# Where the copies of the smaller caches are issued in a decoder step on one core

## What is computed

```
h = RMSNorm(x) * (1 + scale1) + shift1
q_nsa, kv_nsa, g_nsa, qkv_dil, g_merge = split(h @ w_in)
o_nsa, o_dil = NSA attention, dilated attention (three head groups)
m = sigmoid(gA) * (o_nsa @ w_br_nsa) + sigmoid(gB) * (o_dil @ w_br_dil)
x = x + gate1 * (m @ w_out)
h = RMSNorm(x) * (1 + scale2) + shift2
x = x + gate2 * ((silu(h @ w_gate) * (h @ w_up)) @ w_down)
y = RMSNorm_final(x)
```

```
s_win  = concat(cache_win,  new)[:, 1:]   # 8 samples x  512 rows x  256 floats
s_dil1 = concat(cache_dil1, new)[:, 1:]   # 8 samples x  128 rows x 1024 floats
s_dil2 = concat(cache_dil2, new)[:, 1:]   # 8 samples x  512 rows x 1024 floats
s_dil3 = concat(cache_dil3, new)[:, 1:]   # 8 samples x 2048 rows x 1024 floats
```

## Time and profile before

| | |
|---|---|
| median of 3 runs | 2106.77 us (2106.63 to 2110.05) |
| profiled execution | 2110.02 us, of it 2107.7 us span from first to last instruction |
| TensorE busy | 1952.0 us, 93% of the span |
| VectorE, ScalarE busy | 977.2 us (46%), 772.9 us (37%) |
| granted TensorE clock, mean | 0.950 |
| moved by DMA | 512.53 MB, 243 GB/s on average |

### The profile page before, as it was taken

How to read it: one execution, slowest core, us unless ns; L and a number is a source line. 1 busy time by engine, 2 the same in 40 slices (tenths; PEclk the granted TensorE clock), 3 DMA queues, 4 the chain that set the end, 5 groups by cost and what they waited for, 6 DMA issues and landing times.

```text
span 2107.7 us, 36811 instructions
## 1 busy us (share of the span) xinstructions
PE 1952.0 (93%) x15765; PEld 1786.1 (85%) x15765; DVE 977.2 (46%) x1730; ACT 772.9 (37%) x1232; POOL 58.4 (3%) x108
## 2 busy tenths in 40 slices
PE   6988999999879997999999996999999999999967
PEld 3667999999645565699999996999999999999966
DVE  3355445554346532264444756344444433645425
ACT  2345333334324432253333434333333333533322
POOL 0000000000000000000000000000000000000010
PEclk9998989999989959889999997999999999999989
DMA  9981769889899916665555653686767676578791
GB/s 372 422 288 61 214 208 313 280 275 301 338 393 372 412 43 251 229 191 186 180 182 170 219 172 141 235 271 230 267 231 267 233 244 207 196 243 270 249 315 56
DMA packets 336137, 512.53 MB, mean 243 GB/s; under 512 B 8753, under 2 KB 310105, under 8 KB 319497
## 3 DMA queue, kind: packets, MB, share of 16 engines
q1 hardware_dynamic: 316146, 368.53, 52.5%
q0 software_dynamic: 5248, 125.73, 15.1%
q10 hardware_dynamic: 14640, 16.80, 2.4%
HBM read 504.29 MB, written 98.91 MB: 286 GB/s over the span
## 4 chain that ended last, share of the span: by engine, by line
PE 84%; DMA 9%; DVE 4%; ACT 2%; issue 1%; SPq 0%; DVEq 0%; ACTq 0%
PE bank L1129 17%; PE bank L1130 17%; PE bank L1131 17%; PE bank L842 5%; PE bank L843 5%; PE bank L844 5%; DMA piece<-in_w_ada 4%; PE bank L732 3%; PE bank L769 2%; DMA piece<-in_w_down 2%; PE bank L900 2%; PE bank L875 1%; DMA mem<-in_cache_sel_kv,runs 1%; DMA mem<-in_const 1%; PE bank L888 1%; PE bank L960 1%
## 5 line engine op out<-in xcount | busy, mean ns | idle before, releaser
L1129 PE MATMUL bank<-piece,piece 128*128 128x264 f32 x3072 | 877.8, 286 | 50.6 <-DVE piece L2050 26.0
L1130 PE MATMUL bank<-piece,piece 128*128 128x264 f32 x3072 | 877.0, 285 | 0.0
L1131 PE MATMUL bank<-piece,piece 128*128 128x264 f32 x3072 | 876.6, 285 | 0.0
L2055 DVE TENSOR_TENSOR piece<-piece,piece 128x2048 fp32r<-128x2048 f32 (+2 forms) x216 | 440.9, 2054 | 504.5 <-ACT piece L1541 504.5
L1129 PEld LDWEIGHTS bank<-piece,piece 128*128 128x128 f32 x3072 | 582.4, 190 | 52.2 <-DVE piece L2055 24.6
L1541 ACT CAST piece<-piece 128x2048 fp32r<-128x2048 f32 (+2 forms) x216 | 368.7, 1715 | 589.0 <-PE bank L1131 509.6
L1131 PEld LDWEIGHTS bank<-piece,piece 128*128 128x128 f32 x3072 | 582.4, 190 | 0.0
L1130 PEld LDWEIGHTS bank<-piece,piece 128*128 128x128 f32 x3072 | 582.0, 189 | 0.0
L842 PE MATMUL bank<-piece,piece 128*128 128x264 f32 (+1 forms) x816 | 241.1, 295 | 0.0
L843 PE MATMUL bank<-piece,piece 128*128 128x264 f32 (+1 forms) x816 | 234.9, 288 | 0.0
L844 PE MATMUL bank<-piece,piece 128*128 128x264 f32 (+1 forms) x816 | 234.5, 287 | 0.0
(11 more groups left out here) (324 smaller groups left out, 1449.7 us busy)
## 6 DMA issues: line engine op xcount, KB each, us to landing
piece<-in_w_ada SPq DMA_DIRECT2D x48, 2048.0 KB, 12.3
out_s_dil<-in_cache_dil_kv POOLq DMA_DIRECT2D x64, 1023.5 KB, 6.3
piece<-in_w_in SPq DMA_DIRECT2D x50, 1024.0 KB, 8.2
piece<-in_w_gate SPq DMA_DIRECT2D x22, 2048.0 KB, 8.1
piece<-in_w_up SPq DMA_DIRECT2D x22, 2048.0 KB, 8.1
piece<-in_w_down SPq DMA_DIRECT2D x32, 1408.0 KB, 6.7
piece<-in_w_in SPq DMA_DIRECT2D x16, 2048.0 KB, 8.2
piece<-in_w_out SPq DMA_DIRECT2D x8, 2048.0 KB, 8.7
```

What stands on the lines that cost most here:

```text
L1129: mm(out, w_high[:, k, :], half_tile(x_high[k]), start=(start and k == first_tile), stop=False)
L1130: mm(out, w_high[:, k, :], half_tile(x_low[k]), start=False, stop=False)
L1131: last = mm(out, w_low[:, k, :], half_tile(x_high[k]), start=False, stop=(stop and k == len(x_high) - 1))
L2055: v.tensor_tensor(half_chunk(a, k_tiles, f, CW), raw, half_chunk(buffer, k_tiles).bitcast(F32), ALU.subtract)\
```

## The change

GpSimd's list of copies is put in another order, with other waits. The `dil2` copies come directly behind the selected gathers, and the copy of sample c waits for `mg_half` 1 + 6c, the first half of iteration c of the merge. Then come `dil1` and `win`, those of sample c together, at `wo_half` 1 + 2c in the output projection. The second half of `dil3` comes last, with the waits in the feed-forward that it had. The down projection has no copies left. Number, size and content of the copies stay.

```
         selected_gathers()
+        for c in range(B):
+            for z, a in copies("dil2", 512, c):
+                pool.wait_ge(mg_half, 1 + 6 * c)
+                pool.dma_start(z, a).then_inc(*caches_copied.mark(by=16))
+        for c in range(B):
+            pool.wait_ge(wo_half, 1 + 2 * c)
+            for name, n in (("dil1", 128), ("win", WIN)):
+                for z, a in copies(name, n, c):
+                    pool.dma_start(z, a).then_inc(*caches_copied.mark(by=16))
         for c in range(B // 2, B):
             for eighth, (z, a) in enumerate(copies("dil3", 2048, c, 8)):
                 pool.wait_ge(ff_half, 2 + (8 * (c - B // 2) + eighth) * 84 // 32)
-                pool.dma_start(z, a).then_inc(*caches_copied.mark(by=16))
-        for c in range(B):
-            for z, a in copies("dil2", 512, c):
-                pool.wait_ge(dn_half, 1 + 7 * c)
-                pool.dma_start(z, a).then_inc(*caches_copied.mark(by=16))
-        for name, n in (("dil1", 128), ("win", WIN)):
-            for c in range(B):
-                for z, a in copies(name, n, c):
-                    pool.dma_start(z, a)\
-                        .then_inc(*caches_copied.mark(*(("all",) if (name, c) == ("win", B - 1) else ()), by=16))
+                pool.dma_start(z, a).then_inc(*caches_copied.mark(*(("all",) if (c, eighth) == (B - 1, 7) else ()), by=16))
```

## The result

Measured beside the kernel before on the same chip, the changed kernel takes 2088.46 us in the median against 2108.41: ratio 0.9904, 95% interval 0.9886 to 0.9922. That is 20.0 us, and the forecast gain was 20.8 us. The forecast of 2086.0 us had been made from a median of 2106.77; with more executions the kernel before stands at 2108.41, so most of the 2.5 us between forecast and result is the starting point. The profiled execution has a span of 2089.6 us instead of 2107.7.

A forecast was written before the change was run, and what follows sets the result against it. TensorE bounds the kernel, stalled once by a late w_down load behind a burst of copies. Removing 18.42 us idle and 2.37 us slow clock, with zero added elsewhere, takes 2106.77 to 2086.0 us; range 2083 to 2094.

The forecast's parts named there:

- The removed stall: Late down projection: TensorE's 18.42 us idle behind one late w_down load and 2.37 us of slow clock go, gain 20.8 us.
- The burst as the cause: Down projection: the unspaced last dil2, eight dil1 and eight win copies from 2007.95 us made one w_down load take 39.21 us.
- The third rival: Nothing changes: the late down-projection load has another cause, or copies run elsewhere than written; 2106.8 us, chance 0.03.
- Merge: Eight dil2 copies added in the merge cost zero; upper bound 1 us in each of seven iterations, 7 us.
- The pattern iteration: Merge iteration of 32.1 us taken as typical: slot 1 slack 6.3 us, copy landing 7.6 us before the next slot 1 load.
- The limit of 16.1 us: Merge: TensorE waits once a slot 1 load takes over 9.8 + 6.3 = 16.1 us.
- The price of a full meeting: A load issued together with a dil2 copy takes 6.3 us longer, read in the down projection as 13.0 instead of 6.7.
- Output projection: A dil1 and win pair after every second half costs zero, upper bound 2 us; DMA share some 0.81.
- The slower rival: Merge: a stretched copy delays slot 1 loads past the limit; at 22 us a loss of 41 us, 2127 us, chance 0.03.
- The starting point: Whole kernel: forecast set from the three-run median 2106.77 us, 3.3 lower than the profiled execution's 2110.0.
- Two readings that were off: TensorE had three prepared halves after 2007.83 us; a pause of some 10 us after the merge covers the eighth copy's meeting.

The follow-up runs named there:

- e7: The changed kernel with the dil2, dil1 and win copies left out, so their old rows are missing from the output; ratio 0.9878 to the kernel before.
- e10: The kernel before, burst in place, with dil1 and win copies cut into 128 rows of about 4 KB instead of 16 of 32 KB; ratio 0.9999.
- e11: The kernel before, burst in place, with dil1 and win copies cut into 256 rows of about 2 KB; ratio 1.0009.
- e9: The kernel before with one wait more: the burst of 16 copies is issued at dn_half 58, after the last w_down load; ratio 0.9861.
- e3: The kernel before with all small copies kept in the down projection but spaced, dil2, dil1 and win of one sample together at dn_half 1 + 7c; ratio 0.9886.
- e2: The kernel before with only dil2 moved to the merge; all 16 dil1 and win copies stay a burst at dn_half 50; ratio 0.9966.
- e8: Against the kernel before: dil2 in the merge, dil1 spaced in the output projection, eight win copies in a burst at dn_half 50; ratio 0.9902.
- e5: The changed kernel with dil2 copies waiting for mg_half 4 + 6c, each issued together with the slot 1 load; ratio 0.9909 to the kernel before.
- e6: The changed kernel with dil2, dil1 and win copies of one sample together at mg_half 4 + 6c in the merge; ratio 1.0168 to the kernel before.
- e1: The kernel before with only dil1 and win moved, in pairs, to the output projection; dil2 stays in the down projection; ratio 0.9899.
- e4: The changed kernel with all 16 dil1 and win copies in a burst at wo_half 1 in the output projection; ratio 0.9893 to the kernel before.
- e12: The kernel before with each dil1 and win copy made of two copies taking alternate 2 KB pieces, 32 instead of 16 in the burst; ratio 1.0041.

## Why the prediction was right

- **The removed stall**: 18.42 us of idle time and 2.37 us of slow clock, together 20.8. The profiles give 21.1 in the down projection and the norm, and 20.0 from the first merge load to the end. The difference is the 1.2 us of the clock at the start of the output projection, which e7, e10 and e11 show to be apart from the copies and from the change. No load was late next: 7.8 us at most, 6.7 in the median.
- **The burst as the cause**: forecast from the order of issue and the queues' bytes. e9 and e3, which change only when copies are issued within the down projection, remove the whole stall; e2 and e8 scale the delay of the load with the bytes. The third rival is dead.
- **Merge**: a cost of zero forecast, zero measured (e7). The pattern iteration's timing held: in the kernel after, the slot 1 loads beside the copies arrived after 8.1 to 9.3 us; the copy was over before. The slot 0 loads, forecast at 10.8, took 8.6 to 9.7, because the copies landed after 8.1 us and so met them for some 2.5 us instead of 4.1. The limit of 16.1 us is 15.8 by e5 and e6. The price of a full meeting, 6.3 us, was about right too: 6.7 at most in e1.
- **Output projection**: zero forecast, and a DMA share of 0.81 against 0.78 measured. It has far more room than the change uses (e4).
- **The slower rival** was a true mechanism with the right threshold. Its price in the prediction counted idle time only (7 x 5.9 at 22 us, 41 us); with the clock after each stall, 2.1 us, it would have been 56. e6, at 21.2 us in the mean, lost 52.
- **The starting point**: I set the forecast on a median of three and left open whether the 3.3 us to the profiled execution were a longer stall. As far as the profiles show they are not. The kernel before has one profile, but e10 and e11, its repeats up to the down projection, have the same time from the merge to the end within 0.6 us, and their first merge load is issued at 886.3 and 888.9 us: the spread arises before the merge.
- **Two readings that were off** without touching the sum: from 2007.83 to 2031.8 TensorE worked through six halves (three slots) of weights, not three; and between merge and output projection it pauses 2.91 us, not some 10. The first `w_out` load, which meets the eighth copy, landed after 9.5 us, near 1154, and was wanted at 1168, so it needed no pause to cover it.

What the page on copies in the Trainium skill (DMA: Bandwidth & Descriptors, section "Anatomy of one DMA — SWDGE (gpsimd) path") gives for this size, 6.8 us as an estimate, is nearer to the 8.1 us measured in the merge than my 9.9, which came from a stage where every copy met a load, four of the eight from its start. It changed nothing in the sum.

The change was thus larger than its effect: three reorderings, of which a single wait (e9), the spacing in place (e3) or the pairs alone (e1) would each have done. As the kernel without the small copies is no faster than the changed one, no better version was left to look for in their placement.

## What to carry to other kernels

Price background copies by the bytes that are in flight when the tightest load is issued, whichever was issued first, and compare with the time until the consumer needs that load: here some 3.1 us per MB on top of the load's own landing, against 20.8 us in the down projection, 31 (estimated) in the output projection and 15.8 in the merge. The price is not the same everywhere: in the merge, beside the branch loads, e6 comes to 4.1 us per MB (21.2 less 8.2, over 3.14). Below the limit a placement is free, above it each microsecond counts once and TensorE's slow restart counts on top. Look at the end of a queue's list first: transfers that stand there without a wait of their own all start together, and putting them behind the last load is the cheapest repair.

## What the hardware showed beyond that

- A queue can block its issuer. In the burst before, SyncE's third load of the iteration, begun at 2023.93, occupied the queue's sequencer for 20.73 us, where the others took 0.37. The third load did the same in e10, e11, e2 and e12, for 20.4, 19.1, 13.5 and 11.4 us. In the kernel before the fourth load was therefore issued only at 2044.8, 13 us after its slot had come free. In the kernel after no issue of L609 took over 0.383 us.

```profile
L609 SPq DMA_DIRECT2D piece<-in_w_down x32: 368/373/20727, 1764.5 to 2044.8; - x32
```

```profile
L609 SPq DMA_DIRECT2D piece<-in_w_down x32: 368/373/383, 1767.5 to 2034.9; - x32
```

- The same share of the DMA engines' time can move very different amounts. In e12 the copies in alternate pieces of 2 KB went at first as fast as the long rows of the kernel before, and later, when only `win` copies and loads were left, at two thirds of that, with the engines just as busy. The cause stays open. Two stretches of e12, and one of the burst in the kernel before (last two columns: DMA share, GB/s):

```profile
2012.00:2040.00 28.00, 23.14 (x190) 22.93 (x189) 5.65 (x4) 5.33 (x5) 16.31 (x32) 0.97 1.01 314
2040.00:2052.00 12.00, 10.10 (x66) 9.89 (x66) 2.38 (x2) 0.46 (x1) 0.00 (x0) 0.79 1.02 201
```

```profile
2012.00:2046.00 34.00, 19.79 (x163) 19.58 (x161) 3.25 (x2) 2.48 (x2) 4.09 (x9) 0.84 0.96 311
```

- The same short pause can cost a slow stretch or not. Between the merge and the output projection TensorE idles 2.91 us in each of the fourteen kernels; the first matmul after it then ran at the higher level in e1 and at the lower, 1.2 GHz, in the kernel after:

```profile
1168.25 0.36 PE L1129 MATMUL bank<-piece,piece 128*128 128x264 f32 x1 [2.91 <-DVE piece L2050]
```

```profile
1168.10 0.56 PE L1129 MATMUL bank<-piece,piece 128*128 128x264 f32 x1 [2.91 <-DVE piece L2050]
```
